# Gathers on GpSimd that carry the wait for their ring place, without the increment that stood behind it

## What is computed

```python
q = (xb @ w_q).reshape(PEER_BLOCK, PEER_HEADS, 2, D_HALF)
s1, s2 = ...                       # scores against two sets of 128 keys
top_s, sel = lax.top_k(cand, 16)   # 8 heads x 16 experts for each token
eidx = jnp.take_along_axis(cidx, sel, axis=-1)
g = jax.nn.softmax(top_s, axis=-1)
u = u_tab[eidx]                    # 16384 experts, rows of 1024 float32
act = jax.nn.gelu(jnp.einsum("thkd,td->thk", u, xb))
return jnp.einsum("thk,thkd->td", g * act, v_tab[eidx])
```

## Time and profile before

| what | value |
|---|---|
| time, median of 3 runs | 1827.37 us (1826.25 to 1831.63) |
| the profiled execution: its own time / its span | 1829.08 us / 1826.9 us |
| busy PE / DVE / POOL / ACT | 1470.6 / 1427.7 / 783.3 / 634.3 us |
| moved by DMA | 675.78 MB, mean 370 GB/s |
| of it by GpSimd's queue | 538.39 MB, 75.3% of 16 engines' time |

### The profile page before, as it was taken

One profiled execution on the slowest core, in us unless ns is written; L12 is line 12 of the kernel. 1 busy time (PEld: TensorE's weight loads), 2 busy tenths in 40 slices (PEclk: granted clock), 3 DMA queues, 4 the chain that ended last, 5 costly groups with the idle time before them and its releaser, 6 DMA issues.

```text
span 1826.9 us, 17538 instructions
## 1 busy us (share of the span) xinstructions
PE 1470.6 (80%) x4706; PEld 800.0 (44%) x4706; DVE 1427.7 (78%) x3039; ACT 634.3 (35%) x1935; POOL 783.3 (43%) x667
## 2 busy tenths in 40 slices
PE   6799796666675651976868998999998888999997
PEld 5485343433342221633745655433334555433332
DVE  1277788999898778689998989996668888666666
ACT  4335534222222221340136776221115667311112
POOL 2023223476776668857733434222223443322220
PEclk9899898878877785988989999999999888999998
DMA  9389999899999999999978989999998999999996
GB/s 356 146 334 410 375 354 382 336 397 399 398 384 399 368 416 361 372 357 388 405 277 307 353 335 358 418 416 417 416 418 351 345 366 370 383 417 417 417 416 263
DMA packets 146482, 675.78 MB, mean 370 GB/s; under 512 B 15216, under 2 KB 15472, under 8 KB 97232
## 3 DMA queue, kind: packets, MB, share of 16 engines
q0 software_dynamic: 92832, 538.39, 75.3%
q1 hardware_dynamic: 50496, 132.68, 18.9%
q10 hardware_dynamic: 3056, 3.61, 0.6%
HBM read 671.61 MB, written 3.01 MB: 369 GB/s over the span
## 4 chain that ended last, share of the span: by engine, by line
PE 32%; DMA 29%; DVE 19%; issue 10%; ACT 7%; POOL 2%; DVEq 0%; POOLq 0%; SPq 0%
DMA arena<-experts 18%; DMA ring<-experts,idc 10%; PE pb L1479 9%; PE accY L1494 8%; DVE ring L921 5%; PE pb L1299 4%; DVE ring L910 3%; PE pb L1468 2%; PE pb L1308 2%; PE pq L1425 2%; ACT arena L1224 2%; DVE arena L970 2%; PE pb L1317 2%; PE pb L1324 2%; POOL ring L621 1%
## 5 line engine op out<-in xcount | busy, mean ns | idle before, releaser
L619 POOL DMA_INDIRECT ring<-experts,idc x384 | 437.6, 1140 | 889.7 <-DVE xt L930 387.7
L910 DVE CUSTOM_DVE_ANT_0 ring<-ring,h 128x1024 f32<-128x1024 f32 x384 | 466.2, 1221 | 202.2 <-DMA ring<-experts,idc 201.4
L1494 PE MATMUL accY<-ring,diag 128*128 128x512 f32 x792 | 459.6, 717 | 203.9 <-ACT diag L1210 203.7
L1479 PE MATMUL pb<-arena 128*128 128x512 f32 x1024 | 473.5, 608 | 19.1 <-DMA arena<-experts 12.2
L621 POOL DMA_INDIRECT ring<-experts,idc x256 | 335.5, 1311 | 110.7 <-issue 77.1
L1199 ACT ACTIVATE ge<-zt 128x1 f32<-128x1 f32 x384 | 76.4, 199 | 779.4 <-DVE zt L910 778.1
L1494 PEld LDWEIGHTS accY<-ring,diag 128*128 128x128 f32 x792 | 161.2, 221 | 415.0 <-ACT diag L1210 277.0
L1479 PEld LDWEIGHTS pb<-arena 128*128 128x128 f32 x1024 | 186.9, 191 | 304.1 <-issue 197.4
L930 DVE SCALAR_TENSOR_TENSOR xt<-ring,coef,xt 128x1024 f32<-128x1024 f32 x186 | 238.2, 1281 | 6.8 <-ACT coef L1203 6.7
L921 DVE CUSTOM_DVE_ANT_0 ring<-ring,arena 128x1024 f32<-128x1024 f32 x128 | 153.4, 1220 | 11.5 <-DMA ring<-experts,idc 10.4
L921 DVE CUSTOM_DVE_ANT_0 ring<-ring,h 128x1024 f32<-128x1024 f32 x128 | 151.7, 1223 | 11.8 <-DMA ring<-experts,idc 10.9
(11 more groups left out here) (178 smaller groups left out, 1082.9 us busy)
## 6 DMA issues: line engine op xcount, KB each, us to landing
arena<-experts SPq DMA_DIRECT2D x128, 512.0 KB, 15.1
arena<-w_q SPq DMA_DIRECT2D x12, 2048.0 KB, 19.5
arena<-w_in SPq DMA_DIRECT2D x11, 2048.0 KB, 20.9
ring<-experts,idc POOLq DMA_INDIRECT x640, 9.2
arena<-w_out SPq DMA_DIRECT2D x4, 2048.0 KB, 20.6
ring<-w_out SPq DMA_DIRECT2D x2, 2048.0 KB, 20.0
xt<-x_all SPq DMA_DIRECT2D x5, 512.0 KB, 13.5
y_all<-xt ACTq DMA_DIRECT2D x5, 512.0 KB, 3.5
```

The costliest lines, as they stand in the source:

```text
L619: nc.gpsimd.indirect_dma_start(ring[:, at // 2], None, experts, index).then_inc(gat[at], 16)
L910: V.tensor_tensor_reduce(out=half(g), in0=half(g), in1=h2[:], scale=1.0, scalar=0.0, op0=ALU.mult, op1=ALU.add, accum_out=zt[:, s % 8:s % ...
L1479: ins = T.matmul(pb[:, 2 * j + k], cm[:, i, j * P:(j + 1) * P], vring[:, n % VRING, k * 512:(k + 1) * 512], start=i == 0, stop=i == BLOCKS ...
L1494: ins = T.matmul(accY[:, j], diag[:, (n - 1) % DIAGS], ring[:, place, D + j * 512:D + (j + 1) * 512], start=first, stop=final)
```

## The change

One line goes. The wait for the ring place stays as it was, on the same semaphore and for the same value. With nothing between it and the gather, it becomes part of the gather's own instruction.

```diff
                 if k % per == 0:
                     pool.wait_ge(idx_ready, ROUND_BASE[f] + k // per + 1)
                     pool.sem_inc(pool_held, 1)
                 if lay:
                     freed(pool, lay)
-                    pool.sem_inc(pool_held, 1)
                 index = bass.IndirectOffsetOnAxis(ap=idc[:, IDX_PLACE[t], k:k + 1], axis=0)
```

## The result

| comparison | changed kernel, median | before, median | ratio | 95% interval |
|---|---|---|---|---|
| first, 5 runs each | 1811.57 us (1810.17 to 1813.34) | 1826.25 us | 0.9925 | 0.9899 to 0.9951 |
| second (f1) | 1816.23 us | 1826.39 us | 0.9946 | 0.9923 to 0.9968 |
| third (h3) | 1816.97 us | 1824.45 us | 0.9959 | 0.9945 to 0.9974 |

The changed kernel is faster in every comparison. The first says 14.7 us, which lies just outside my range (1813 to 1832). The three together say (0.0075 + 0.0054 + 0.0041) / 3 = 0.57%, or 10.3 us. That is inside the range, but it is 2.6 times my 3.9 us, and above the 0.3% that I had called no change. Single executions of either kernel scatter by up to 10 us around their median, so a difference of a few us between two single profiles means little here. The comparisons of many runs carry the argument.

A forecast was written before the change was run, and what follows sets the result against it. DMA engines were taken as full in most stages, GpSimd not bound by its own work. Five flights at 0.55 us (2.75) plus four at half (1.1) gave 3.9 us: 1827.37 - 3.9 = 1823.5 us, range 1813 to 1832.

The forecast's parts named there:

- The delay: From a release to the waiting gather's start on GpSimd: 0.55 of 0.79 us saved, about 0.24 us left.
- Rival A: GpSimd's sequencer holds the gather until its release, so only 0.2 us is saved in all: 1827.2 us, chance 0.26.
- The increment costs nothing between queued gathers: GpSimd's 0.30 us gap belongs to the gather; the gather ahead (0.94 us) covers the increment, so removing it saves nothing there.
- The block stages count zero: 118 of 142 waits for VectorE fall there; the chain runs over blocks and DMA engines are full, so no gain.
- rival C: Earlier gathers stretch the v table's block flights on the chain in the block stages: slower, 1836 us, chance 0.11.
- So it is no bound by its own work: GpSimd is busy for only 783.3 of 1826.9 us, so only the delay from release to gather start can matter.
- my own first sentence: Opening of the prediction: read the stretches first, because the averages of the page hide the stages.
- The nine flights between 470 and 720 count zero: Nine of the chain's 20 gather flights lie where DMA engines are full; starting them earlier gains nothing.
- Rival B: Flights from 470 to 720 also shorten, filling small DMA holes; all 18 behind releases give 9.9 to 13.0 us, chance 0.21.
- Nine flights in the stages with slack: Chain flights behind releases outside 470 to 720: five at 0.55 us, four from 290 to 470 at half, 3.9 us.
- 0.55 + 1.1 = 1.65 us: One flight between 107 and 290 in full, 0.55 us, and four between 290 and 470 at half, 1.1 us.
- B's upper price: A gain of 13.0 us, from 18 flights behind releases at 0.72 us each; the range's lower end was to hold it.

The follow-up runs named there:

- f1: The changed kernel, unaltered, measured a second time; 0.9946 of the kernel before, 1816.23 us.
- h3: The changed kernel, unaltered, measured a third time; 0.9959 of the kernel before, 1816.97 us.
- e1: Kernel before with its 634 increments moved behind the gathers, so each gather carries its wait; 0.9963 of the kernel before, 1818.86 us.
- h1: Changed kernel with the increment back for the 131 gathers of the two block stages alone; 0.9943 of the kernel before.
- f3: Kernel before with each increment replaced by three chained small GpSimd memsets, the gather waiting for the last; 1.0383 of the kernel before.
- g1: Kernel before with twenty increments behind each wait instead of one; 1.0601 of the kernel before.
- e4: Kernel before with seven increments behind each wait instead of one; 1.0013 of the kernel before, 1828.5 us.
- h2: Changed kernel with increments back for gathers of about 107 to 470, 940 to 1140 and 1395 to 1568 us alone; 0.9991 of the kernel before.

## Why the prediction was wrong, point by point

**The delay: right.** The working gave 0.55 us off 0.79, with 0.24 left. Measured are 0.54 us off 0.796, with 0.258 left. Rival A is refuted: the sequencer's part is done while the wait is open. The Trainium skill ("Perfetto Trace Analysis", section "Per-engine timelines") has a software-generated DMA wait in a queue behind the sequencer, with the sequencer ready for the next instruction. The trace agrees with the first half, by the 0.26 us of the changed kernel. It doesn't bear out the second: in e1 the increment behind a gather runs only 0.03 us after that gather's release.

**The increment costs nothing between queued gathers: right with one exception.** The gap of 0.30 us stayed. But of the 25 gathers of the mixed stage that lost time, eight were released less than about 0.5 us before the gather ahead of them ended, and for these the cover is partial. My sum had no term for them.

**The block stages count zero: right.** h1 has the increments back there and takes the changed kernel's time. The blocks' median flight stayed at 15.1 us, so rival C didn't occur either.

**"So it is no bound by its own work": the step that failed.** I took GpSimd's 783.3 us of 1826.9, an average over the span, in spite of my own first sentence. The row of the stage itself stood in the earlier trace rows: 176.22 us of 250, 135 gathers, to which 135 x 0.30 = 40 us of fixed gaps belong. That makes 217 of 250 us, 87%. What is added to GpSimd there comes out for the greater part as time (52.2 of 72 us in f3), and nothing of it in the block stages. That the real increments cost through this, and not in another way, is argued from f3 and g1; e4 doesn't fit it.

**The nine flights between 470 and 720 count zero, because the DMA share is 1.00: failed too.** The share of 1.00 did not mean that earlier requests only stand in line: under it a DMA engine was idle for 5.2 us on average. With increments in this stage alone 0.36% of the time (6.6 us) come back, though only 0.16% against e1. Rival B was nearest, with nearly the right price (11.5 us against 10.3 on average). Whether the gain there comes by its small holes in the DMA engines or by GpSimd's nearly full sequence, the runs don't separate; the rise to 403 GB/s, which would have spoken for B's holes, did not recur. I gave it 0.21 because a share of 1.00 spoke against it.

**Nine flights in the stages with slack, 3.9 us: too small.** h2 lost 0.32% against h3 (5.8 us) and 0.48% against the mean. 3.9 us would be 0.21%. For the part from 107 to 470 us I had 0.55 + 1.1 = 1.65 us, and the way to gather 137 became 4.9 us shorter. That a delay counts in these stages was right, and its size was not. A likely reason is that the flights on one chain leave out those on paths just beside it; no run tests that. For the range, I let B's upper price end at 1813 and left nothing for the spread from one comparison to the next, which moved the measured gain from 7.5 to 14.7 us.

## What to carry to other kernels

When an instruction of its own does the waiting, the sequencer's work on the gather behind it comes after the release. Let the instruction that needs the data carry the wait; here it was worth 0.57% on the DMAs issued from GpSimd. To see whether an engine may bound a stage, add its fixed gaps to its busy time in that stage alone. Don't take a DMA share of 1.00 for proof that earlier requests are worth nothing, and don't read a difference of a few us in one stage from a single pair of profiles.

## What the runs showed of the hardware

- A gather on GpSimd starts 0.258 us after its release when it carries the wait, and 0.796 us after it when a separate instruction waited; both hardly vary. In e1 the increment behind a gather that waits runs 0.03 us after that gather's release in 233 of 246 cases, and before it in none. Each further increment on the sequencer adds 0.078 us ((1.27 - 0.80) / 6).
- A small memset on GpSimd between two queued gathers makes their gap 0.40 us instead of 0.30 us, and three in a row, each waiting for the last, 0.73 us.
- The summed share of the DMA engines' busy time can pass 1 (1.01 at 403 GB/s), because packets overlap: more than 16 were under way on the 16 engines, by 4.8 us an engine. At a share of 1.00, 5.2 of 250 us were idle.
- Added delay costs in an uneven way (0.57%, then 0.13%, then 5.9% for 0.54, 0.47 and 1.0 us). The large last part comes with a sequencer that needs longer for each gather (2.1 us) than a short gather takes (1.24 us); why the middle part is so small is open.
- The busy time of the same 167 gathers varies between executions, from 205.4 to 220.4 us in the kernels without memsets and with at most one increment for each gather.
